# Hybrid S5 and mixture-of-experts step: expert body written once, latent state outputs in halves, two pieces of a linear unit in free slots

## The reference

```python
mod = silu(cond) @ w_ada + b_ada                 # (1024) @ (1024, 6144): shifts, scales, gates
h = rms_norm(x, norm_mix) * (1 + sc1) + sh1
u = h @ w_in                                     # 64 groups of 16 channels
y = u * d_skip
for d in range(2):                               # forward and backward
    x_re, x_im = u_g @ Bbar                      # 64 complex states per group
    h_re, h_im = associative_scan(...)           # latent scans start from given states
    y = y + h_re @ c_re - h_im @ c_im
val, gate = split(gelu(y) @ w_glu, 2)            # (1024) @ (1024, 2048)
x = x + g1 * val * sigmoid(gate)
h = rms_norm(x, norm_ffn) * (1 + sc2) + sh2
scores = sigmoid(h @ router_w)                   # 16 experts in 4 groups: best group, top 2 in it
a = silu(h @ w_gate[e]) * (h @ w_up[e])          # each (1024, 1024)
x = x + g2 * sum_over_top2(weight * a @ w_down[e])
y = rms_norm(x, norm_final)                      # also returned: final context states
```

## Time and profile before

| | |
|---|---|
| median of 3 runs | 878.7 us (877.99 to 882.97) |
| profiled execution, its own time | 875.71 us |
| its span, first to last instruction | 873.9 us |
| TensorE busy | 747.5 us (86%) |
| VectorE, ScalarE, GpSimd busy | 301.5, 184.7, 63.4 us |
| transfers | 259.23 MB, mean 297 GB/s |
| mean granted clock of TensorE | 0.915 of full |

### The profile page before, as it was taken

How to read it: one execution, slowest core, us unless ns; L and a number is a source line. 1 busy time by engine, 2 the same in 40 slices (tenths; PEclk the granted TensorE clock), 3 DMA queues, 4 the chain that set the end, 5 groups by cost and what they waited for, 6 DMA issues and landing times.

```text
span 873.9 us, 22646 instructions
## 1 busy us (share of the span) xinstructions
PE 747.5 (86%) x9627; PEld 410.4 (47%) x9628; DVE 301.5 (34%) x860; ACT 184.7 (21%) x386; POOL 63.4 (7%) x98
## 2 busy tenths in 40 slices
PE   5799785698969984979999999999999999998840
PEld 5355462085554444445445545535535554455320
DVE  3789789995004215021112112201201211120117
ACT  3554242001023222020212012112102212120213
POOL 1000002900010000300000000000000000000000
PEclk9889896657999995989999999999999999999985
DMA  9900429940018039599999999999999999999924
GB/s 346 406 6 1 193 97 420 320 182 4 10 44 276 20 127 402 202 386 364 410 410 409 410 410 409 410 410 410 411 410 409 411 410 410 410 410 410 409 104 165
DMA packets 70015, 259.23 MB, mean 297 GB/s; under 512 B 10728, under 2 KB 10776, under 8 KB 65864
## 3 DMA queue, kind: packets, MB, share of 16 engines
q1 hardware_dynamic: 66968, 254.02, 73.6%
q0 software_dynamic: 1632, 3.20, 1.0%
q10 hardware_dynamic: 1360, 1.19, 0.6%
HBM read 252.49 MB, written 6.29 MB: 296 GB/s over the span
## 4 chain that ended last, share of the span: by engine, by line
issue 53%; DVE 3%; POOL 3%; POOLq 2%; DMA 1%; ACT 0%; SPq 0%; DVEq 0%
POOL y_scratch L491 1%; POOLq L509 1%; POOL slot_list L465 1%; DMA a4r<-slot_list 1%; DMA ring<-y_scratch 0%; DVE ring L1571 0%; DVE sreg L1560 0%; DVE sreg L1561 0%; DVE sreg L1562 0%; POOL pool_tick L479 0%; DMA y_scratch<-vreg,sidx 0%; POOL sidx L484 0%; ACT sreg L746 0%; POOLq L508 0%; POOLq L497 0%
## 5 line engine op out<-in xcount | busy, mean ns | idle before, releaser
L1097 PE MATMUL ps<-ring,vreg 128*32 128x512 f32 x2240 | 247.2, 597 | 18.6 <-issue 11.6
L1097 PEld LDWEIGHTS ps<-ring,vreg 128*32 128x32 f32 x2240 | 72.8, 110 | 185.8 <-issue 171.9
L1119 PE MATMUL ps<-ring,vreg 128*32 128x256 f32 x2240 | 124.2, 380 | 0.0
L1082 PEld LDWEIGHTS ps<-vreg,sreg 128*128 128x128 f32 x816 | 96.5, 197 | 15.1 <-issue 13.4
L1082 PE MATMUL ps<-vreg,sreg 128*128 128x96 f32 x816 | 100.2, 281 | 1.5 <-DVE vreg L1491 1.5
L1521 DVE TENSOR_TENSOR vreg<-vreg,ps 128x256 f32<-128x256 f32 x48 | 17.3, 417 | 229.3 <-ACT vreg L720 229.3
L1119 PEld LDWEIGHTS ps<-ring,vreg 128*32 128x32 f32 x2240 | 71.2, 110 | 46.8
L1005 PE MATMUL ps<-ring 128*128 128x512 f32 x192 | 84.9, 603 | 2.2 <-ACT vreg L692 0.8
L1532 DVE COPY vreg<-ps 32x256 f32<-32x256 f32 x96 | 40.7, 424 | 105.8 <-PE ps L1119 103.3
L732 ACT ACTIVATE vreg<-ps 32x256 f32<-32x256 f32 x96 | 35.9, 374 | 145.2 <-PE ps L1119 143.2
L720 ACT ACTIVATE vreg<-ps 128x256 f32<-128x256 f32 x48 | 15.0, 384 | 216.1 <-PE ps L1097 216.1
(11 more groups left out here) (255 smaller groups left out, 571.9 us busy)
## 6 DMA issues: line engine op xcount, KB each, us to landing
ring<-in_moe_w_gate SPq DMA_DIRECT2D x128, 512.0 KB, 13.7
ring<-in_moe_w_up SPq DMA_DIRECT2D x128, 512.0 KB, 15.0
ring<-in_moe_w_down SPq DMA_DIRECT2D x128, 512.0 KB, 13.2
ring<-in_w_ada SPq DMA_DIRECT2D x24, 1024.0 KB, 12.2
ring<-in_ssm_w_glu SPq DMA_DIRECT2D x8, 1024.0 KB, 11.7
ring<-in_ssm_w_in SPq DMA_DIRECT2D x8, 512.0 KB, 21.7
ring<-y_scratch SPq DMA_DIRECT2D x6, 512.0 KB, 6.5
tmat<-ada_rows SPq DMA_DIRECT2D x4, 512.0 KB, 10.5
```

The source lines that it names most:

```text
L1082: last = pe.matmul(bank[:, col * CAP:(col + 1) * CAP], h2[:, t, k * P:(k + 1) * P], onehot[:, t, :], start=(t == 0), stop=(t == NT - 1))
L1097: last = pe.matmul(ps[t][32 * j:32 * j + 32, :], xgT[:, k, 32 * t:32 * t + 32], w[:, :, 256 * j:256 * j + 256], start=(k == 0), stop=(k == ...
L1119: last = pe.matmul(ps[3 + t // 2][32 * dj:32 * dj + 32, 256 * (t % 2):256 * (t % 2) + 256], aT[:, t, c2, 32 * j:32 * j + 32], ring[:, KT + ...
```

## The change

It has six parts.

1. Late pieces: slots by the table `LATE_SLOTS`. Pieces 12 and 13 go to slots 0 and 1 once `u_c` has been transposed (`pe_uT` 8); pieces 14 to 17 wait for piece n-5, the upper half of `w_glu` follows, then the last six pieces. TensorE works off six pieces before the kernel parts.
2. The latent `y_inside` follows the context's, ahead of the context's `y_state`; the gate rows are loaded after it as before (`pe_inside` is now 3). Banks 0, 1 and 2 to 5 are exchanged for this, and the final states' transposes use the banks of the context's y and wait for its GELU.
3. The latent `y_state` runs in halves, each between pieces of the linear unit's parts 0 and 1.
4. Parts 4 and 5 (the last token tile) are computed together, weight unit by weight unit, each followed by `glu_free`; the transposes of h2 of tile 0 move to after part 2.
5. Units 0, 1 and 3 of expert 0 are loaded after `pe_yT` 6, units 8 to 11, 4 to 7 and 2 as `glu_free` counts.
6. TensorE's expert body stands once: the third tile's gate and up products and its down products are under `pe.If(count > 64)`, ahead of those of the other two tiles, which free the units. The third tile is always transposed.

```diff
+LATE_SLOTS = (4, 5, 6, 7, 0, 1, 4, 5, 6, 7, 4, 5, 6, 7, 4, 5)
...
             sp.wait_ge(pe_u, 6)
-            for n in range(KT, 3 * KT):
-                b, k = divmod(n, KT)
-                if n == 2 * KT:
-                    sp.wait_ge(pe_p, 32)
-                    for kk in range(4, KT):
-                        load_glu(kk)
-                if n >= KT + 4:
-                    sp.wait_ge(pe_ada, n - 3)
-                sp.dma_start(ring[:, 4 + n % 4, :], ...
-            for k in range(4):
-                sp.wait_ge(pe_ada, 2 * KT + k + 5)
+            for n in range(KT, KT + 4):
+                late_piece(n)
+            sp.wait_ge(pe_uT, 8)
+            for n in range(KT + 4, KT + 6):
+                late_piece(n)
+            for n in range(KT + 6, KT + 10):
+                sp.wait_ge(pe_ada, n - 5)
+                late_piece(n)
+            sp.wait_ge(pe_p, 32)
+            for k in range(4, KT):
+                load_glu(k)
+            for n in range(KT + 10, 3 * KT):
+                sp.wait_ge(pe_ada, n - 3)
+                late_piece(n)
+            for k in (2, 3, 0, 1):
+                sp.wait_ge(pe_ada, 2 * KT + (5 + k if k > 1 else 7 + k))
                 load_glu(k)
...
-            for u in range(2):
+            for u in (0, 1, 3):
                 load_unit(u, 0)
-            sp.wait_ge(pe_glu, 12)
-            for u in range(2, NU):
+            for n, u in enumerate((8, 9, 10, 11, 4, 5, 6, 7, 2)):
+                sp.wait_ge(glu_free, min(n + 1, KT))
                 load_unit(u, 0)
...
-                    act.wait_ge(pe_glu, 2 * m + 2)
+                    if m < 4:
+                        act.wait_ge(pe_glu, 2 * m + 2)
+                    else:
+                        act.wait_ge(glu_free, KT)
...
+                    if m == 2:
+                        store_h2T(0)
...
-                if t == 1:
-                    store_h2T(0)
...
-            y_inside(lambda i: ps[i], range(16), CTX0, CC).then_inc(pe_inside, 1)
+            y_inside(ctx_bank, range(16), CTX0, CC).then_inc(pe_inside, 1)
+            pe.wait_ge(act_ada, 2)
+            for f in range(2):
+                y_inside(lambda i: lat_bank(f, i), lat_blocks(f), LAT0, CL).then_inc(pe_inside, 1)
             pe.wait_ge(dve_scan, 1)
             pe.wait_ge(pe_inside, 1)
-            y_state(lambda i: ps[i], range(16), CTX0, CC)
+            y_state(ctx_bank, range(16), CTX0, CC)
+            pe.wait_ge(act_gelu, 2)
...
+            glu_part(0, range(4, KT))
+            pe.wait_ge(ld_glu, 16 * 4)
+            glu_part(0, range(4))
+            pe.wait_ge(dve_scan, 2)
+            lat_state(0)
+            glu_part(1, range(4, KT))
+            lat_state(1)
+            glu_part(1, range(4))
+            lat_channels(0)
+            lat_channels(1)
...
+            for k in tuple(range(4, KT)) + tuple(range(4)):
+                for m in (4, 5):
+                    for part in range(2):
+                        col = part * D + (m % 2) * 512
+                        last = pe.matmul(ps[GLU_BANK[m] + part][:, :], yT_lat[:, k, P:2 * P],
+                                         ring[:, 4 + k, col:col + 512], start=(k == 4), stop=(k == 3))
+                last.then_inc(glu_free, 1)
...
+                if count is None:
+                    third_gate_up(it)
+                else:
+                    with pe.If(count > 64):
+                        third_gate_up(it)
                 for k in range(KT):
                     pe.wait_ge(ld_unit[k], it * 32 + 32)
...
+                    gate_up(k, 0)
+                    gate_up(k, 1).then_inc(unit_free, 1)
...
+                if count is None:
+                    third_down(it)
+                else:
+                    with pe.If(count > 64):
+                        third_down(it)
                 for kk in range(KT):
+                    if kk % 2 == 0:
+                        pe.wait_ge(ld_unit[KT + kk // 2], it * 32 + 32)
+                    down(kk, 0)
+                    last = down(kk, 1)
...
             with pe.Fori(0, NE) as e:
                 n = pe.value_load(counts[0:1, bass.ds(e, 1)], min_val=0, max_val=T)
-                with pe.If(n <= 64):
-                    expert(e, e, 2)
-                with pe.If(n > 64):
-                    expert(e, e, TT)
+                expert(e, e, n)
```

126 lines of the change are left out of this document (63 added, 63 removed).

## The result

The changed kernel takes 868.59 us (median of 4 runs, 865.46 to 869.81), beside 878.35 us for the kernel before on the same chip (873.85 to 882.97): a ratio of 0.988, with a 95% interval of 0.9841 to 0.9919. In a later set, timed again with the last experiments, it took 866.45 us beside 879.45, a ratio of 0.9858 (0.9825 to 0.9891). So it is faster by 10 to 13 us, and the forecast was 6.7 us faster.

What follows compares the result with a forecast made beforehand. The expert phase was taken as bound by its weight stream at 410 GB/s, behind a chain in front. Terms -5.1 + 3.5 + 0.6 - 3.2 - 2.5 = -6.7 us from 878.7 gave 872.0 us, range 863 to 879.

Steps and rivals of the forecast that it cites:

- Two pieces earlier: Conditioning's late pieces: two loaded in an idle queue end the saturated stretch sooner, -5.1 us (2 if TensorE's pace takes over).
- rival D: Front and loop: gain hidden by another wait (copies into `tmat`), loop as before, 878 us; chance 0.2 together with rival B.
- The latent part inside a chunk: Latent `y_inside` ahead of the context's state outputs: 128 records move to clock 0.50 and take 7.5 us, +3.5 us.
- Final states after the GELU: Final states' two transposes, once hidden in TensorE's wait for ScalarE, now share its banks and follow it: +0.6 us.
- Halves of the latent states: Latent states between linear unit parts: about half of 6.9 us of "issue" stalls goes, -3.2 us (0 to -6.9).
- rival A: Faster still: interleaving removes all stalls, or moved matmuls find the clock up; 865 to 868 us, chance 0.2.
- The tail of the linear unit and the early loads: Linear unit's end: same wide matmuls, and earlier expert 0 loads were already covered by the routing; 0 us.
- The expert once: Expert loop: the 6.45 us stall before expert 1, taken as a long jump's price, goes; -2.5 us.
- the third tile ahead: Experts 4, 7 and 9: units freed later, but 1.9 us of reserve keeps the weight stream from running dry; 0 us.
- rival B: Stalls stay or move, stream loses about 2 us after expert 9; 877 to 880 us, chance 0.2 together with rival D.
- Rival C: Expert loop: jumps over the third tile cost time in every two-tile expert; 885 to 898 us, chance 0.1.
- sign of "wrong": Signs against: loop "issue" rows of 1 us or more, DMA share under 1 after experts 4, 7 or 9, stalling small matmuls.

Runs made afterwards that it cites:

- bodies in the other order: The changed kernel with two expert bodies again, the three-tile body written first and the two-tile body last: 868.91 us, 0.9904 of the kernel before.
- pieces as before: The changed kernel with late pieces in their old slots and order: 866.7 us; the same with the third tile under short conditions inside each unit: 867.64 us.
- y_inside later: The changed kernel with the latent `y_inside` back behind the linear unit's part 0: 866.93 us, 0.9878 of the kernel before.
- states together: The changed kernel with both halves of the latent `y_state` in one run behind the linear unit's parts 0 and 1: 873.25 us, 0.9942 of the kernel before.
- the loads late: The changed kernel with all but two of expert 0's unit loads after the whole linear unit: 868.03 us, 0.9888 of the kernel before.
- either loop: The changed kernel with its own single-body loop (868.59 and 866.45 us), or with the two-body expert loop of the kernel before (869.42 us).

## Why the prediction was right or wrong

Forecast and measurement agree in sign and in the range (863 to 879), and the time, 868.6 us, lies 3.4 us under the 872.0 of the forecast. That it comes so near is in part luck. The largest term, -5.1, brought 2 us at most, +3.5 came to about nothing and -3.2 to twice as much: three errors of about 3 us, of which the first offsets one of the others. For the front as a whole the forecast was -4.2 us at the start of expert 0, and the means below give -9.3.

The front, stretch by stretch, from the profiles of all kernels (means, us; bodies in the other order included, with its stall of 3.3 us; the columns are the three profiles with the front of before, the seven with the whole changed front, and the single edits):

| from, to | before's front | changed front | pieces as before (2) | y_inside later | states together |
|---|---|---|---|---|---|
| start of y_inside | 178.4 | 176.4 | 178.5 | 177.1 | 177.5 |
| to the linear unit | 28.0 | 33.3 | 32.2 | 28.6 | 33.6 |
| to its third part | 56.3 | 45.1 | 43.9 | 50.1 | 51.3 |
| to expert 0 | 95.1 | 93.7 | 94.1 | 94.2 | 94.6 |
| expert 0 starts | 357.9 | 348.6 | 348.8 | 349.9 | 357.0 |

The stretch to the third part goes from 43.6 to 47.1 us within the seven, mostly by the clock: the first 32 wide records take 13.97 us in one profile and 17.03 in another. So differences of under 2 us to a single profile say little.

*Two pieces earlier*, -5.1: the step failed. I took the saturated stretch to end 5.1 us sooner because the DMA share was 1.00. The share did not stay at 1.00, since TensorE comes to the pieces later through the longer gaps in the kernel parts. The lower bound that I named, "2 if the pace of TensorE takes over", is what came: 2.0 us at `y_inside`, and at expert 0 nothing that can be told (348.6 against 348.8). The copies into `tmat`, which I kept for rival D as "no row here shows", are now what ends that wait, from 0.29 to 0.77 us.

*The latent part inside a chunk*, +3.5: the step failed. In front it came to 4.7 us instead of 7.5 (33.3 less 28.6), and behind the linear unit's part 0 it freed 4.9 (50.1 less 45.1, where 0.59 us of stop stands in the run that it lengthens), so the term is about 0 (-0.2, by one profile). The assumption that failed is "I count on no recovery": the clock rose within the longer run, at about 185 us. The rule of the Trainium skill that I set against it (TensorE: Matmul & The Clock Gate, "What's actually happening") gave 0 for this term. The traces agree with it where the latent matmuls stand in the run, and disagree over the 21 us of the earlier trace rows and the same code in three other profiles, where it stays at 0.50 without a pause.

*Final states after the GELU*, +0.6: right, as far as one profile tells. With the latent part out of the way the stretch to the linear unit is 28.6 against 28.0 us.

*Halves of the latent states*, -3.2: too small by half. The stretch to the third part is 51.3 us with the halves together and 45.1 with them apart: -6.1, of which the small matmuls alone show 4.7 to 5.1 (20.8 less 15.7 to 16.1). Of the three cases that I named, the first nearly held, "if the supply of instructions catches up in between, all 6.9 go". The reserve of about 245 records that the earlier trace rows showed is refilled during 7.1 us of wide matmuls: both runs of 256 pass without a stop, in the eight other profiles with the latent `y_inside` moved and the halves apart too, while a run lengthened by its 128 records stops after 277 (the kernel with it back in place). One stop of 1.0 to 1.5 us stays, in `y_channels`. This is rival A's mechanism; 866.4 us lies in its range and 868.6 just above it.

*The tail of the linear unit and the early loads*, 0: right, as far as can be told. The stretch to expert 0 is 94.2 us in the kernel before and 94.0 in the changed one (first profiles), and 94.1 with the loads late.

*The expert once*, -2.5, and *the third tile ahead*, 0: the first was right in itself and the second failed. The stall went with the long jump, and its end brings 3.4 us of stream. But "1.9 us are left: just enough" was wrong: the stream ran dry after expert 9 (2.4 us in the changed kernel's profile), as rival B had it ("about 2 us"), and after expert 4 too (1.8 us), which I had not reckoned. The reckoning had TensorE at expert 9 3.6 us earlier than before, counted from expert 0; it was not 0.2 us earlier (275.08 against 275.23 us). I had subtracted "some 3 us" for the waits of the third tile, which demands all eight units within 7 us. At expert 4 alone they are 1.28 + 1.50 + 0.91 = 3.7 us, from an estimate of 2.3, and the lower clock behind them, for which I had no term, costs another 3.4 us. Together the two terms are -2.1 us by the loop's length (466.2 against 468.3), and nothing that can be told by the times of the change with either loop (868.6 and 866.4 against 869.4).

Rival C did not come: no short jump stops TensorE, neither 2 an expert nor 12. The rule that stood beside it (the Trainium skill, Runtime: NRT & Kernel Launch, "Instruction fetch mechanics") has such a stop for each taken branch out of the code already fetched. The traces agree for the long jumps that stopped, the first time each; what had been fetched at the one into expert 4, with 0.62 us, no run here shows. Rival B's two parts about the stalls are refuted one by one, by the other order of bodies and by the run with the halves together. Rival D is refuted for the front as a whole, though its copies do hide what the earlier pieces could have brought.

Of the signs that I named, expert 0 near 352 us (350.6), the third part near 258 (256.6) and a gap under 1 us before expert 1 (0.26) came. `y_inside` at 172 us (175.8), the latent matmuls at 55 to 62 ns and clock 0.50 (37 ns, clock up), and no window under 400 GB/s did not, and one sign of "wrong" came: a DMA share of 0.83 and 0.79 after experts 4 and 9.

The sum by what was measured: -2.0 at the start of `y_inside`, +5.3, -11.2 and -1.4 in the three stretches that follow, -2.1 in the loop: -11.4 us, beside -9.8 and -13.0 by the medians.

## What to carry to other kernels

A long train of small matmuls that stops for "issue" can be split: two runs of 256 with 7 us of wide matmuls between them take no stop, where one run of 512 and more, with the clock up, loses some 5 us, and it is an edit of two lines. A long jump, where it stops the engine, does so only once, so the body is worth taking out only if that one stop stands on the path, and the code that takes its place must not free buffers later: here the gain of 3.4 us was paid back with 1.5 to 4.5 us by the order in which the ring was freed. And where a stretch is bound by its transfers, ask what TensorE must have done before each of them may start, since the share of 1.00 was lost as soon as TensorE came later.
